# A kernel of ten transformer stages on one core: side steps ahead of the splits, one wait fewer at the eights' turns, and the first stage turning all of x before its tiles

## The chip, the cores and the metric

One core of a Trainium2 chip runs the whole program in one launch. The metric is the device time of an execution in microseconds (us). Three executions of the kernel before took 2540.09, 2541.14 and 2547.57 us; the median is 2541.14.

## The reference

x is 256 rows of 1024 float32 numbers. Two blocks work on it, of two layers each.

```python
def first_block(x, ...):          # DEPTH = 2
    for i in range(DEPTH):
        h = swiglu(rms_norm(x, g[0]), ffn_w_gate[i, 0], ffn_w_up[i, 0], ffn_w_down[i, 0])
        x = x + 0.5 * rms_norm(h, g[1])
        hm = rms_norm(x, g[2])
        m = dilated_attention(hm, ...) if i == 0 else retention(hm, ...)
        x = x + rms_norm(m, g[3])
        h = swiglu(rms_norm(x, g[4]), ffn_w_gate[i, 1], ffn_w_up[i, 1], ffn_w_down[i, 1])
        x = x + 0.5 * rms_norm(h, g[5])

def second_block(x, mem, ...):    # two layers
    for l in range(DEPTH):
        dq, dk, dv, c_q, c_kv_kr, xq, gate_logits = jnp.split(rmsnorm(x, g_mix[l]) @ w_in[l], ...)
        y_diff = diff_attention(dq, dk, dv, ..., diff_lambda[l], ...) @ w_diff_o[l]
        y_mla = latent_attention(c_q, c_kv_kr, ...) @ w_mla_o[l]
        y_mem = memory_cross_attention(xq, rmsnorm(mem, mem_gain[l]) @ w_mem_kv[l], ...) @ w_cross_o[l]
        merged = gates[:, :, 0] * y_diff + gates[:, :, 1] * y_mla + gates[:, :, 2] * y_mem
        x = x + merged @ w_out[l]
        x = x + jnp.square(jax.nn.relu(rmsnorm(x, g_mlp[l]) @ w_mlp1[l])) @ w_mlp2[l]
```

The dilated attention has 16 heads of 64 in three groups: the first is dense over a band, the second and third attend within classes of equal position modulo the dilation. The differential attention subtracts `lam` times its second map, and `lam` is computed from the small vector `diff_lambda`. The retention has 4 heads, each normed over its 512 values. All products are of float32 quality.

## The kernel before

**Tiles.** The weights are read in 744 tiles of 128 x 1024 float32 (512 KB). SyncE (SP) loads a tile into one of four raw buffers (L1504, L1511). ScalarE (ACT) rounds it to w_hi (L1780). VectorE (DVE, L2060), and in the mix stages every second time GpSimd (POOL, L2724), makes the rest, w_lo. TensorE (PE) then runs 12 matmuls of 512 columns for the tile: w_hi by x_hi, w_lo by x_hi, w_hi by x_lo, each four times (L1555 to L1557; L1579 to L1581 for blocks that go chunk by chunk). x itself is turned by PE in pieces of 128 (L1599) and divided into hi (ACT, L1806, L1808) and lo (DVE, L2086, L2088) in the same way.

**The plan.** The order of all work is written out once, as a list of steps, by Python generators. Every engine's program walks this one list and takes its part of each step, in order; an engine never passes a waiting instruction. The steps that matter here:

- `("mm", i)` and `("mm_chunk", i)`: PE's matmuls of tile i.
- `("split", i)`: ACT's w_hi and then w_lo of tile i, with SP's load of tile i+4. w_hi of tile i waits for the end of tile i-4 on PE, whose buffer it takes; the load of tile i+4 waits for w_lo of tile i.
- side steps: turning x or the heads, norms, rotations, scores, softmax, values. `drive(main, side)` runs one tile of `main` and then one group of side steps, in turn; `main` is a stage's projections. A tile's generator (`block()`, L552, and `block_by_chunk()`, L567) yields once a tile, and at that yield the side group is written into the list.
- `evac`: the result of a block is taken out of PSUM once its last tile is done.

`tile_used(i)` (L531) writes `("split", i + 4)`, or keeps it back while a stage ends. `second_part` is a function that the feed of a stage leaves behind: `block()` calls it after the stage's second tile.

**Stages.** ffn, dilated attention, ffn, ffn, retention, ffn, then mix, mlp, mix, mlp. `feed()` (L645) opens each: gains times x into `tok` (L2068), turned by PE, then rows' squares for the norm (ACT L1832). In its first half (`first`) it turns columns 0 to 511 of both halves of the rows, in the second (`second`) the others.

**The eights.** In the dilated stage the groups with classes go by eight heads (`by_classes()`, L915): scores on PE, softmax on DVE (L2260 to L2268) and ACT (exponential, L1905), den, the sum of the exponentials, on DVE (L2286), turns of the probabilities on PE (L1691), values on PE (L1711), weights and weighing, then `combine` and turns into `da_out_hi` (ACT L1806) and `da_out_lo` (DVE L2086). Two eights are interleaved. In the list den stands behind the softmax of the next half of the eight.

**Retention.** While the gates' and the output's tiles run, each head's values are normed with a chain DVE (L2430 to L2436), POOL (L2705), ACT, DVE (L2444).

**The prelude** (L1194) of a mix stage runs beside the last tiles of the stage ahead of it: the memory block and the small vectors are read by POOL's queue (L2819, L2825), then `lambda` computes lam on DVE and ACT (L2598 to L2604, L2019), and so on.

Of the kernel before, what the change touches and what calls it, by code (L numbers as in the profile page):

```python
# [49 lines left out]
RAW, SPLIT = 4, 4  # L50
# [339 lines left out]
class Kernel:  # L390
# [161 lines left out]
    def block(self, xt, w, rows, c0, n, first=0):  # L552
        view = w.rearrange("(k p) n -> p k n", p=P)
        chunks, per = rows // P, TILE // n
        b = self.new_block(xt, first, chunks, n)
        for k0 in range(0, chunks, per):
            nk = min(per, chunks - k0)
            self.tiles.append(Tile(view[:, k0:k0 + nk, c0:c0 + n], nk, n, b, k0))
            self.step("mm", len(self.tiles) - 1)
            self.tile_used(len(self.tiles) - 1)  # L560
            if self.second_part and len(self.tiles) == self.second_part[0]:
                self.second_part[1]()
                self.second_part = None
            yield
        return b

    def block_by_chunk(self, xt, w, rows, turned):  # L567
        view = w.rearrange("(k p) n -> p k n", p=P)
        b = self.new_block(xt, 0, rows // P, D)
        for k in range(rows // P):  # L570
            while not turned(k):
                yield
            self.tiles.append(Tile(view[:, k:k + 1, :], 1, D, b, k))
            self.step("mm_chunk", len(self.tiles) - 1)
            self.tile_used(len(self.tiles) - 1)
            yield
        return b

    def by_turns(self):
# [65 lines left out]
    def feed(self, between=None, order=""):  # L645
        st, g = self.st, self.next_gain()
        self.xt = Transposed(f"x{st}", *self.xt_parts)
        self.xt_scaled = True
        gained = {}

        def part(half, c):
            if self.pending:
                self.pending(half, c)
            by = "pool" if c and between else "dve"
            self.step("gain", st, half, c, by, g, [self.x_event[half][c]] + self.tok_after[half])
            gained[half, c] = "gain", st, half, c

        def turned(half, c):
            self.feed_turned = self.turn(lambda h, s: self.tok[:, h, s * P:(s + 1) * P], self.xt, half, [(4 * c + j, 4 * c + j) for j in range(4)],
                                         [gained[half, c]], self.xt_after, order=order)  # L660

        def first():
            turned(0, 0)
            turned(1, 0)

        def second():
            part(0, 1)
            part(1, 1)
            self.release(1)
            if between:  # L670
                between()
                first()
            turned(0, 1)
            turned(1, 1)
            self.release()
            self.pending = None
            self.step("next_gain", g + 2, list(gained.values()))
            self.tok_after = [[self.feed_turned]] * HALVES
            for half in range(HALVES):
                self.step("rows", st, half, list(self.x_event[half]), self.stat(2), self.stat(1), self.stat(1), "row_natural" if order else "row_scale")  # L680

        part(0, 0)
        part(1, 0)
        if between:
            second()
        else:
            first()
            if not self.tiles:
                for i in range(SPLIT):
                    self.split(i)  # L690
            self.second_part = len(self.tiles) + 2, second

    def last_tile(self):
# [828 lines left out]
def pe_program(k):  # L1522
    pe, q, ev = k.nc.tensor, Queue(k.nc.tensor), k.ev
# [8 lines left out]
    for what, *of in k.plan:  # L1532
# [6 lines left out]
        if what == "mm":  # L1539
            i, = of  # L1540
            t = k.tiles[i]
            b, hi, lo = t.block, k.w_hi[i % SPLIT], k.w_lo[i % SPLIT]
# [5 lines left out]
            for half in range(HALVES):  # L1548
                bank = banks.held["blk", b.uid, half][:, 0:t.n]
                for j in range(t.nk):  # L1550
# [6 lines left out]
                    mm = pe.matmul(bank, xl, wh, start=False, stop=(c == b.chunks - 1))  # L1557
# [6 lines left out]
        if what == "mm_chunk":  # L1564
            i, = of
            t = k.tiles[i]
            b, hi, lo = t.block, k.w_hi[i % SPLIT], k.w_lo[i % SPLIT]
# [5 lines left out]
            for c in range(2):  # L1573
                cols = slice(c * BLOCK, (c + 1) * BLOCK)
                for half in range(HALVES):
# [5 lines left out]
                    mm = pe.matmul(bank, xl, hi[:, cols], start=False, stop=(t.k0 == b.chunks - 1))  # L1581
# [6 lines left out]
        if what == "turn":  # L1588
# [9 lines left out]
            for j, (c, s) in enumerate(t.chunks):  # L1598
                mm = pe.transpose(bank[:, j * P:(j + 1) * P], src(t.half, s), order)  # L1599
# [4 lines left out]
        if what == "turn_heads":  # L1604
# [5 lines left out]
            for h in range(t.n):  # L1610
                for half in range(HALVES):
                    z = t.src(half, t.h0 + h)
                    at = h * SEQ + half * P
                    mm = pe.transpose(bank[0:z.shape[-1], at:at + P], z, order)  # L1614
# [51 lines left out]
        if what == "oct_scores":  # L1666
            o, = of
# [16 lines left out]
        if what == "oct_turn":  # L1684
            o, b = of
            bank = yield from bank_for("oct_turn", o.uid, b)
            q.wait_ge(*(yield from ev.of("oct_exp", o.uid, b)))
            q.wait_ge(*(yield from ev.of("oct_den", o.uid, b)))
            p = k.probs.held["oct", o.uid, b]
            for m in range(OCT // 2):  # L1690
                mm = pe.transpose(bank[:, m * P:(m + 1) * P], p[:, m * P:(m + 1) * P], k.ident[:, :])  # L1691
            mm.then_inc(*ev.mark(k.pe_done, ("oct_read", o.uid, b)))
            k.probs.give(ev.at["oct_read", o.uid, b], "oct", o.uid, b)
# [1186 lines left out]
```

## Time and profile before

| what | value |
|---|---|
| executions, median | 2540.09, 2541.14, 2547.57; 2541.14 us |
| the profiled execution | 2539.82 us, span 2538.5 us |
| mean granted TensorE clock | 0.982 |
| PE busy | 2421.2 us, 95% of the span, 11746 instructions |
| PE weight loads | 1957.6 us, 77% |
| DVE busy | 1480.2 us, 58% |
| ACT busy | 1194.4 us, 47% |
| POOL busy | 281.5 us, 11% |
| DMA | 411.36 MB, mean 162 GB/s |
| w_lo on DVE (L2060) | x688, 837.9 us, mean 1222 ns |
| w_lo on POOL (L2724) | x56, 134.3 us, mean 2399 ns |
| w_hi on ACT (L1780) | x744, 781.0 us, mean 1053 ns |

PE's matmuls overlap by their durations, so the distance of their starts, not the duration, is what one costs. The granted clock is a share of the full 2.4 GHz. An idle time in brackets is how long the engine had done nothing, with the instruction that ended it.

### The profile page before, as it was taken

How to read it: one execution, taken by the hardware profiler on the slowest of the kernel's cores; microseconds unless marked ns; L12 is line 12 of the kernel's file. 1: busy time of each engine (PE TensorE's matmuls, PEld its weight loads, DVE VectorE, ACT ScalarE, POOL GpSimd, SP SyncE). 2: the span in 40 equal slices, each digit the busy share in tenths (PEclk: the TensorE clock that was granted, in tenths of full speed). 3: DMA queues.
4: the chain of work that ended last, by engine and by line, in shares of the span. 5: the costliest groups of instructions: out<-in, count | busy, mean ns of one | idle time of the engine just before them, and what ended most of it. 6: DMA issues, size and time to landing. Idle time of an engine off the chain costs nothing.

```text
span 2538.5 us, 29689 instructions
## 1 busy us (share of the span) xinstructions
PE 2421.2 (95%) x11746; PEld 1957.6 (77%) x11746; DVE 1480.2 (58%) x2158; ACT 1194.4 (47%) x1754; POOL 281.5 (11%) x248
## 2 busy tenths in 40 slices
PE   7998999989999999999999999999999999999999
PEld 5786777768877877777787787777787877887787
DVE  4555556675555547766554577655565576645653
ACT  4443454344434445444444465554554455554543
POOL 1100010000000000000001112333101122333000
PEclk9998999989999999999999999999999999999999
DMA  6765544446556666544566554344556554445554
GB/s 206 204 182 151 175 119 117 144 122 190 175 173 184 181 182 181 160 141 144 176 184 182 181 170 143 108 125 158 179 175 209 179 160 123 117 131 159 169 174 146
DMA packets 211339, 411.36 MB, mean 162 GB/s; under 512 B 13690, under 2 KB 26890, under 8 KB 211200
## 3 DMA queue, kind: packets, MB, share of 16 engines
q1 hardware_dynamic: 204192, 388.55, 51.1%
q0 software_dynamic: 6576, 19.80, 2.9%
q8 instruction: 93, 1.52, 0.2%
q10 hardware_dynamic: 432, 1.11, 0.1%
q14 instruction: 46, 0.38, 0.1%
HBM read 408.31 MB, written 1.10 MB: 161 GB/s over the span
## 4 chain that ended last, share of the span: by engine, by line
PE 81%; DVE 11%; ACT 4%; DMA 2%; issue 2%; POOL 1%; ACTq 0%; DVEq 0%
PE banks L1555 24%; PE banks L1557 23%; PE banks L1556 23%; DVE w_lo L2060 3%; PE banks L1599 2%; ACT w_hi L1780 2%; PE banks L1649 2%; PE banks L1623 1%; PE banks L1634 1%; PE banks L1614 1%; DMA small<-in_diff_lambda 1%; POOL stat L2705 1%; DVE mx_merged L2693 1%; PE banks L1579 1%; PE banks L1580 1%
## 5 line engine op out<-in xcount | busy, mean ns | idle before, releaser
L2060 DVE TENSOR_TENSOR w_lo<-w_raw,w_hi 128x1024 fp32r<-128x1024 f32 x688 | 837.9, 1222 | 862.0 <-ACT w_hi L1780 859.2
L1780 ACT ACTIVATE w_hi<-w_raw 128x1024 fp32r<-128x1024 f32 (+2 forms) x744 | 781.0, 1053 | 974.6 <-PE banks L1557 922.5
L1555 PE MATMUL banks<-w_hi,xt_hi 128*128 128x512 f32 (+3 forms) x2112 | 848.2, 402 | 20.7 <-DVE xt_lo L2088 10.3
L1556 PE MATMUL banks<-w_lo,xt_hi 128*128 128x512 f32 (+3 forms) x2112 | 823.3, 390 | 0.0
L1557 PE MATMUL banks<-w_hi,xt_lo 128*128 128x512 f32 (+3 forms) x2112 | 822.5, 389 | 0.0
L1555 PEld LDWEIGHTS banks<-w_hi,xt_hi 128*128 128x128 f32 x2112 | 403.6, 191 | 111.3 <-issue 18.3
L1557 PEld LDWEIGHTS banks<-w_hi,xt_lo 128*128 128x128 f32 x2112 | 402.3, 190 | 89.1
L1556 PEld LDWEIGHTS banks<-w_lo,xt_hi 128*128 128x128 f32 x2112 | 403.6, 191 | 83.1 <-issue 3.1
L2705 POOL TENSOR_TENSOR stat<-stat,minus_half 128x1 f32<-128x1 f32 (+2 forms) x60 | 54.6, 916 | 1052.4 <-DVE stat L2147 731.3
L2724 POOL TENSOR_TENSOR w_lo<-w_raw,w_hi 128x1024 fp32r<-128x1024 f32 x56 | 134.3, 2399 | 304.4 <-ACT w_hi L1780 304.3
L1555 PE MATMUL banks<-w_hi,ffn_ht_hi 128*128 128x512 f32 x352 | 141.9, 403 | 3.3 <-DVE w_lo L2060 3.3
L1557 PE MATMUL banks<-w_hi,ffn_ht_lo 128*128 128x512 f32 x352 | 140.5, 399 | 0.0
L1556 PE MATMUL banks<-w_lo,ffn_ht_hi 128*128 128x512 f32 x352 | 140.5, 399 | 0.0
L1555 PE MATMUL banks<-w_hi,mlp_ht_hi 128*128 128x512 f32 x256 | 102.2, 399 | 1.2 <-DVE w_lo L2060 1.2
L1557 PE MATMUL banks<-w_hi,mlp_ht_lo 128*128 128x512 f32 x256 | 101.5, 396 | 0.0
L1556 PE MATMUL banks<-w_lo,mlp_ht_hi 128*128 128x512 f32 x256 | 101.4, 396 | 0.0
L1555 PEld LDWEIGHTS banks<-w_hi,ffn_ht_hi 128*128 128x128 f32 x352 | 67.0, 190 | 19.5 <-DVE w_lo L2060 3.7
L1557 PEld LDWEIGHTS banks<-w_hi,ffn_ht_lo 128*128 128x128 f32 x352 | 67.0, 190 | 16.4
L1556 PEld LDWEIGHTS banks<-w_lo,ffn_ht_hi 128*128 128x128 f32 x352 | 67.1, 191 | 15.8
L1599 PE MATMUL banks<-ident,tok 128*128 128x128 f32 x212 | 35.2, 312 | 39.4 <-DVE tok L2068 39.4
L1867 ACT ACTIVATE probs<-probs,mx_nmax 128x256 f32<-128x256 f32 x96 | 42.9, 448 | 63.0 <-DVE mx_nmax L2205 62.8
L1599 PEld LDWEIGHTS banks<-ident,tok 128*128 128x128 f32 x212 | 28.0, 159 | 47.1 <-issue 30.0
(382 smaller groups left out, 2550.0 us busy)
## 6 DMA issues: line engine op xcount, KB each, us to landing
w_raw<-in_w_mlp SPq DMA_DIRECT2D x128, 512.0 KB, 3.8
w_raw<-in_w_in SPq DMA_DIRECT2D x104, 512.0 KB, 3.7
w_raw<-in_ffn_w_gate SPq DMA_DIRECT2D x88, 512.0 KB, 3.7
w_raw<-in_ffn_w_up SPq DMA_DIRECT2D x88, 512.0 KB, 3.8
w_raw<-in_ffn_w_down SPq DMA_DIRECT2D x88, 512.0 KB, 3.7
w_raw<-in_attn_w_in SPq DMA_DIRECT2D x72, 512.0 KB, 3.8
w_raw<-in_ret_w_in SPq DMA_DIRECT2D x64, 512.0 KB, 3.9
w_raw<-in_ret_w_out SPq DMA_DIRECT2D x16, 512.0 KB, 3.9
```

Source lines behind the costliest of these rows:

```text
L1555: pe.matmul(bank, xh, wh, start=(c == 0), stop=False)
L1556: pe.matmul(bank, xh, wl, start=False, stop=False)
L1557: mm = pe.matmul(bank, xl, wh, start=False, stop=(c == b.chunks - 1))
L1579: pe.matmul(bank, xh, hi[:, cols], start=(t.k0 == 0), stop=False)
L1580: pe.matmul(bank, xh, lo[:, cols], start=False, stop=False)
L1599: mm = pe.transpose(bank[:, j * P:(j + 1) * P], src(t.half, s), order)
L1649: mm = pe.matmul(out[:, at:at + h.dv], pt[:, kh, s, :], h.v(kh), start=(kh == 0), stop=(kh == n_keys - 1))
L1780: act.activation(k.w_hi[i % SPLIT][:, 0:m], k.raw[i % RAW][:, 0:m], ACT.Copy).then_inc(*ev.mark(k.w_hi_made, ("w_hi", i)))
L1867: act.activation(row, row, ACT.Exp, bias=h.nmax[:, s:s + 1], scale=-1.0, accum_out=h.den[:, s:s + 1]).then_inc(*done)
L2060: dve.tensor_tensor(lo, raw, hi.bitcast(F32), ALU.subtract).then_inc(*ev.mark(k.w_lo_made, ("w_lo", i)))
L2705: pool.tensor_tensor(out, mean, k.minus_half[:, 0:n], ALU.pow).then_inc(*ev.mark(k.pool_done, name))
L2724: pool.tensor_tensor(lo, raw, hi.bitcast(F32), ALU.subtract).then_inc(*ev.mark(k.w_lo_pool, ("w_lo", i)))
```

## The change

In the blocks, the split of a tile is no longer written right behind its matmuls, but after the yield, so behind the side steps of that tile. Where `second_part` is called it stays where it was. In `feed()` of the first stage both parts of x are handled, and the rows' squares, ahead of splits 0 to 3 and of tile 0; before, the second part came after the second tile. PE's turn of an eight waits for the exponential alone; before, it waited for den as well.

```diff
--- before.py
+++ after.py
@@ -556,12 +556,16 @@
         for k0 in range(0, chunks, per):
             nk = min(per, chunks - k0)
             self.tiles.append(Tile(view[:, k0:k0 + nk, c0:c0 + n], nk, n, b, k0))
-            self.step("mm", len(self.tiles) - 1)
-            self.tile_used(len(self.tiles) - 1)
+            used = len(self.tiles) - 1
+            self.step("mm", used)
             if self.second_part and len(self.tiles) == self.second_part[0]:
+                self.tile_used(used)
                 self.second_part[1]()
                 self.second_part = None
-            yield
+                yield
+            else:
+                yield
+                self.tile_used(used)
         return b
 
     def block_by_chunk(self, xt, w, rows, turned):
@@ -571,9 +575,10 @@
             while not turned(k):
                 yield
             self.tiles.append(Tile(view[:, k:k + 1, :], 1, D, b, k))
-            self.step("mm_chunk", len(self.tiles) - 1)
-            self.tile_used(len(self.tiles) - 1)
+            used = len(self.tiles) - 1
+            self.step("mm_chunk", used)
             yield
+            self.tile_used(used)
         return b
 
     def by_turns(self):
@@ -683,11 +688,13 @@
         part(1, 0)
         if between:
             second()
+        elif not self.tiles:
+            first()
+            second()
+            for i in range(SPLIT):
+                self.split(i)
         else:
             first()
-            if not self.tiles:
-                for i in range(SPLIT):
-                    self.split(i)
             self.second_part = len(self.tiles) + 2, second
 
     def last_tile(self):
@@ -1685,7 +1692,6 @@
             o, b = of
             bank = yield from bank_for("oct_turn", o.uid, b)
             q.wait_ge(*(yield from ev.of("oct_exp", o.uid, b)))
-            q.wait_ge(*(yield from ev.of("oct_den", o.uid, b)))
             p = k.probs.held["oct", o.uid, b]
             for m in range(OCT // 2):
                 mm = pe.transpose(bank[:, m * P:(m + 1) * P], p[:, m * P:(m + 1) * P], k.ident[:, :])
```

## Rows read from the trace of the kernel before

**Rows 1.** Part 4 of the page, the chain that ended last: its shares by engine.

```profile
PE 81%; DVE 11%; ACT 4%; DMA 2%; issue 2%; POOL 1%; ACTq 0%; DVEq 0%
```

**Rows 2.** The list of waits, all engines: total us, times, longest us.

```profile
ACT w_hi L1780 <- PE banks L1557: 922.5, 582, 7.3
PE banks L1691 <- DVE da_den L2286: 12.5, 4, 4.9
```

**Rows 3.** Timeline at the start: start us, duration us, instruction, [idle before <- releaser].

```profile
16.76 0.80 PE L1555 MATMUL banks<-w_hi,xt_hi 128*128 128x512 f32 x1 [2.89 <-DVE w_lo L2060]
...
27.25 1.97 PE L1599 MATMUL banks<-ident,tok 128*128 128x128 f32 x8 [3.07 <-DVE tok L2068]
29.75 0.62 ACT L1832 ACTIVATE junk<-x 128x512 bf16<-128x512 f32 x1
29.87 0.76 PE L1555 MATMUL banks<-w_hi,xt_hi 128*128 128x512 f32 x1 [0.65 <-DVE xt_lo L2088]
```

**Rows 4.** Timeline of PE, the eights in the dilated stage.

```profile
414.16 0.63 PE L1691 MATMUL banks<-ident,probs 128*128 128x128 f32 x4 [2.88 <-DVE da_den L2286]
...
427.77 0.63 PE L1691 MATMUL banks<-ident,probs 128*128 128x128 f32 x4 [1.44 <-DVE da_den L2286]
...
509.89 1.12 PE L1691 MATMUL banks<-ident,probs 128*128 128x128 f32 x4 [4.87 <-DVE da_den L2286]
...
523.71 0.76 PE L1579 MATMUL banks<-w_hi,da_out_hi 128*128 128x512 f32 x1 [3.87 <-DVE da_out_lo L2086]
```

**Rows 5.** Timeline of DVE, between the last two of these.

```profile
504.69 1.23 DVE L2060 TENSOR_TENSOR w_lo<-w_raw,w_hi 128x1024 fp32r<-128x1024 f32 x1 [1.49 <-ACT w_hi L1780]
...
510.81 1.23 DVE L2060 TENSOR_TENSOR w_lo<-w_raw,w_hi 128x1024 fp32r<-128x1024 f32 x1 [0.98 <-ACT w_hi L1780]
```

**Rows 6.** Timeline of PE, end of the retention stage.

```profile
1188.51 0.39 PE L1579 MATMUL banks<-w_hi,re_yt_hi 128*128 128x512 f32 x1
1188.74 0.39 PE L1580 MATMUL banks<-w_lo,re_yt_hi 128*128 128x512 f32 x1
...
1196.14 0.50 PE L1579 MATMUL banks<-w_hi,re_yt_hi 128*128 128x512 f32 x1 [1.41 <-DVE w_lo L2060]
```

**Rows 7.** Timeline of DVE, end of the retention stage.

```profile
1189.40 1.23 DVE L2060 TENSOR_TENSOR w_lo<-w_raw,w_hi 128x1024 fp32r<-128x1024 f32 x1 [1.79 <-ACT w_hi L1780]
...
1194.86 1.22 DVE L2060 TENSOR_TENSOR w_lo<-w_raw,w_hi 128x1024 fp32r<-128x1024 f32 x1 [1.79 <-ACT w_hi L1780]
```

**Rows 8.** Timeline of PE, end of the last ffn stage, with the first prelude.

```profile
1389.88 0.80 PE L1555 MATMUL banks<-w_hi,ffn_ht_hi 128*128 128x512 f32 x1 [3.29 <-DVE w_lo L2060]
```

**Rows 9.** Timeline of DVE, the same stretch.

```profile
1376.53 1.23 DVE L2060 TENSOR_TENSOR w_lo<-w_raw,w_hi 128x1024 fp32r<-128x1024 f32 x1 [1.59 <-ACT w_hi L1780]
1386.77 0.29 DVE L2598 TENSOR_TENSOR lam_products<-small 128x128 f32<-128x128 f32 x1 [9.01 <-DMA small<-in_diff_lambda]
```

**Rows 10.** Windows of 4 us: busy us (x instructions) by engine, PEclk, DMA share, GB/s.

```profile
1376.00:1380.00 4.00, 4.00 (x19) 3.22 (x18) 1.23 (x1) 1.78 (x2) 2.91 (x6) 1.00 0.96 254
1390.00:1394.00 4.00, 4.00 (x10) 3.14 (x11) 4.00 (x11) 2.74 (x6) 0.00 (x0) 0.50 0.66 203
```

**Rows 11.** Timeline of PE, end of the first mlp stage, with the second prelude.

```profile
1917.97 0.50 PE L1555 MATMUL banks<-w_hi,mlp_ht_hi 128*128 128x512 f32 x1 [1.21 <-DVE w_lo L2060]
```

**Rows 12.** Timeline of DVE, first mix stage, rotation of q.

```profile
1515.23 0.68 DVE L2572 TENSOR_TENSOR tmp<-mx_q,rope_q 128x512 f32<-128x512 f32 x1
...
1522.10 0.68 DVE L2580 TENSOR_TENSOR mx_q<-mx_q,tmp 128x512 f32<-128x512 f32 x1
```

**Rows 13.** Timeline of PE, first mix stage.

```profile
1521.14 0.40 PE L1555 MATMUL banks<-w_hi,xt_hi 128*128 128x512 f32 x1
...
1530.23 0.47 PE L1555 MATMUL banks<-w_hi,xt_hi 128*128 128x512 f32 x1 [1.57 <-DVE mx_k L2531]
...
1581.97 0.52 PE L1634 MATMUL banks<-ident,probs 128*128 128x128 f32 x3 [2.17 <-DVE mx_kcat L2625]
...
1659.53 0.63 PE L1634 MATMUL banks<-ident,probs 128*128 128x128 f32 x4 [1.26 <-ACT probs L1876]
```

## Prediction

> **What bounds the kernel now.** I read the page first, then the waits, then the timelines of each place where TensorE stands still. In the chain of waits [rows 1] the reader is to see that PE carries 81% and that VectorE (DVE) comes next with 11%: nearly all of the span is matmul columns that the change leaves alone, and only places where another engine hands over late can move. In the list of waits [rows 2] two lines matter. ScalarE (ACT) stood 922.5 us before its w_hi, each time for a tile to end on PE. That is no loss by itself, since a split that waits for tile i makes tile i+4, more than 8 us ahead of use. But whatever stands behind such a split on ACT and DVE is held for up to a tile (2.8 us: 12 matmuls, 0.23 us apart [rows 6]), then for ACT's 1.05 us and DVE's 1.22 us. The other line is PE's 12.5 us in four waits for da_den at the eights' turns. All gaps of PE of 0.25 us or more that I found in its timeline add up to about 108 us. Some 41 of these are at the ends of stages, where no side step stands, and 11 at the start before x is there. So what is to be had is some 55 us at most, and I go through these gaps.
>
> **The rule of the change.** The old order is tile i, split i+4, side steps, tile i+1, split i+5. The new one is tile i, side steps, split i+4. Two things follow. A side step is no longer behind split i+4, but it is now followed by split i+4, whose wait (end of tile i) is met earlier than that of split i+5: side chains gain up to 1.05 + 1.22 = 2.3 us of latency, plus what their engine idled for PE. And each w_lo moves behind one more group of side steps: where DVE and ACT are full of side work, w_lo of tile n comes about when w_lo of n+1 came before. In the long ffn and mlp bodies DVE waits for ACT, w_lo has more than 5 us to spare, and I cost the edit at nothing; without that cover each late w_lo would cost its own delay.
>
> **Start** (old: tile 0 at 16.76, a wait of 3.07 for the second half's turns, those 1.97, another 0.65, tile 2 at 29.87 [rows 3]). New: the second half's gains on DVE right after the first half's xt_lo (15.25 to 16.6), turns until 18, their hi and lo until 19.3, ACT's four squares (the first is in [rows 3]; each 0.62 and then 0.19 for its sum, a little overlapped, 3.0 us for four), then w_hi 0 at about 22 to 22.8 and w_lo 0 at 24.1. Tile 0 at 24.1 instead of 16.76; tiles 0 and 1 plus the mended gaps fill that, and tile 3 comes at 34.4 instead of 34.6. **-0.2**, bounds -0.7 (squares ahead of the turns' hi) and +1 (half clock twice).
>
> **Eights in the dilated stage.** All four den waits vanish as named. What is late next? First pair (2.88 and 1.44 [rows 4]): the values of the first eight wait for da_v, which DVE and ACT evacuate at about 433.0, against 434.5 where PE stood: **-1.4** (bounds -4.3, all of it, and +0.5). Second pair: PE is 3.4 us ahead at 488, loses 2.4 of it again at the next scores, which need da_kt (about 495.7 against 496.7), and then goes through the turn at 509.89 [rows 4] without its 4.87. It gains nothing by that, since at 523.71 it waits for da_out_lo anyway, by the same DVE chain: softmax, combine, weights, turns' lo. In that chain DVE idles only 1.49 at 504.69 and 0.98 at 510.81 [rows 5]; no DVE instruction goes away. At best the chain ends 1.0 (earlier scores) + 2.5 (those idles) = 3.5 us earlier. But between these steps now stand w_lo's whose w_hi ACT makes behind an exponential (0.63 + 1.05), which is the same sum as before: **+0.2** (bounds -3.5 and +1.5). The half clock behind 509.89 may go or stay; PE's wait at 523.71 absorbs it. Together -1.2. If DVE's order did not bind, the 12.5 would all come back with about 3.5 of half clock.
>
> **End of retention.** DVE's chain of a head's norm lasts 5.46 us (w_lo 1189.40 to w_lo 1194.86 [rows 7]) and has one w_lo in it. Now tile 346 (PE 1188.51 [rows 6]) gets the place of 1189.40 and is ready at 1190.6; tile 347 (1191.3, twelve matmuls on) that of 1194.86, ready 1196.1; tile 348, which waited 1.41 until 1196.14 [rows 6], is ready at about 1198.5. Less 1.2 that the chain gains at its start, less what is absorbed: **+2.2**, bounds 0 (chain ahead by a whole split) and +3.5 (with the half clock after a longer wait).
>
> **Lambda in the prelude, twice.** DVE's lam_products waits 9.01 us for its DMA until 1386.77 [rows 9]. Ahead of it stood w_lo 1376.53, for tile 409, which PE ran until 1386.6; behind it w_lo of tile 410, for which PE waited 3.29 us, until 1389.88 [rows 8]. Now lambda is ahead of split 409. Queued behind the waiting instruction are then w_lo 409 and, by ACT's lam, w_hi 409, and PE waits for them: tile 409 starts at about 1389.9 and tile 410 a tile later. One tile of 2.8 us more is lost; the half clock is paid in both. Second layer: the wait of 1.21 [rows 11] becomes 4.0, again +2.8, and now it is long enough for what happened after 3.29: granted clock 0.50, which is the level of 1.2 GHz, and 10 matmuls in 4 us instead of 19 [rows 10], at most 2.5 us for a tile, of which I take 2.0. **+7.6**; bounds +3 and +9. The lower one: the load that follows w_lo 409 is held back too, so the DMA may land up to 2.1 us sooner (a tile of 524 KB at 254 GB/s [rows 10]) in each layer. I take none of it: the reading of the memory block (1 MB, issued just before) is in flight beside it in any case.
>
> The DMA share was 0.96 in 1376 to 1380 while lambda was on its way [rows 10]. The Trainium skill, DMA: Bandwidth & Descriptors, section "Issuing engines are not separate DMA queues", says that transfers of all issuing engines end up on the same 16 DMA engines and interleave. By that rule, which the share of 0.96 fits, the withheld load makes lambda earlier by the full 2.1 us in each layer, the second layer's half clock goes as well, and my sum would be about -5 instead of +1.2; by the row alone it stays at +1.2. It would not leave "no change".
>
> **Mix: q and k turning.** Six rotation instructions for each half, two halves from 1515.23 to 1522.10 + 0.68 [rows 12], stand now ahead of a w_lo instead of behind it. Tile 453, at 1521.14 [rows 13], gets its w_lo at about 1522.3: +1.2. Tile 461 in the same manner for k: +1.6. PE waits at 1530.23 (1.57 [rows 13]) and 1558.52 for DVE's mx_k and mx_v, which the same chain brings no later, so most is given back: **+0.6 a layer, +1.2** (bounds -1 and +5).
>
> **Mix attention.** Early gaps (2.17 at 1581.97 [rows 13], 0.52, 1.70) hang on a chain of norms through DVE, POOL and ACT, and lose about one split's latency between them: -1.0 a layer, **-2.0** (bounds -8.8 and +1). Late gaps (five a layer, first 1.26 at 1659.53 [rows 13], sum 3.5) wait for an exponential whose maximum stood behind a w_lo that DVE idled for; a 2.3 us shorter way covers each: -3.2 a layer, **-6.4** (bounds -7 and 0).
>
> **Sum.** -0.2 - 1.2 + 2.2 + 7.6 + 1.2 - 2.0 - 6.4 = **+1.2 us** on the profiled execution (2539.82, span 2538.5), which is 1.3 below the median 2541.14: I add to the median, **2542.3**. Within 0.3% (7.6 us) is about what a measurement of this kernel can't tell from no change.
>
> **Rivals.**
> Gains hold: side work really was held by splits, so the den waits (12.5 + 3.5 half clock), early gaps (8.8) and late gaps (6.4) all go, and lambda costs 3: 3 - 31.2 = -28, some 2513; half of it gives 2527. For: DVE is busy only 58%. Against: DVE is nearly continuous there [rows 5], and da_out_lo, not da_den, is the last wait there. It decides if the wait at 523.71 shrinks below 3.
>
> Late w_lo (the other sign): w_lo behind DMA and DVE chains, lambda 9, retention 3.5, rotations 5, and of the late gaps only half comes back (-3.2), the eights nothing: +14, 2555. For: w_lo's slack [rows 6, 8] is zero already. Against: such places are few. It decides from about 8 us of new PE<-w_lo waits that no gap gives back.
>
> Nothing moves: every freed wait turns into the next one and the lambda DMA lands earlier: 2541, within 1.
>
> **Chances.** Forecast 0.42, nothing 0.13 (together the same: 0.55); gains 0.25; late w_lo 0.20. Range: 2527 to 2552, one in ten beyond each end; the forecast's own is 2535 to 2548.
>
> **What would show it.** After: no waits PE<-da_den, but a wait of PE for da_out_lo of about 8 us near 523, and one for da_v or values near 433; PE waiting for w_lo about 6 us near 1387 and 4 near 1915, with half clock after both; two or three short waits near 1190 to 1198; the five late gaps of each mix layer gone; tile 0 at 24.1. Wrong would be: the wait for da_out_lo not longer than 4 (gains hold), lambda's wait ahead of no tile, or new w_lo waits in the bodies.

## The result, and the profile after

The changed kernel takes 2530.03 us (median of 4 executions, 2527.24 to 2531.84) against 2542.35 for the kernel before: ratio 0.995, 95% interval [0.9935, 0.9966], so 12 us or 0.5% faster. Run again later as an experiment of its own it gave 2531.00 us and 0.9953 [0.9939, 0.9967]. The forecast was no change (2542.3, with 0.25 for faster). The time is inside the range of 2527 to 2552, but it moved 12 us down where 1.2 us up was forecast.

The profiled execution after took 2531.84 us (span 2530.5), 8.0 less than the profiled one of before. It is the slowest of its kernel's four, and that of before (2539.82) lies 2 us below the medians of that kernel (2541.49 to 2542.35 in all comparisons): this is where the other 4 us are. So the two traces can account for 8 us of the 12. The chain of waits has moved a little from PE [rows 1] to the other engines:

```profile
PE 2417.6 (96%) x11746; PEld 1958.9 (77%) x11746; DVE 1484.7 (59%) x2158; ACT 1189.6 (47%) x1754; POOL 285.0 (11%) x248
...
PE 79%; DVE 12%; ACT 5%; issue 1%; DMA 1%; POOL 1%; ACTq 0%; DVEq 0%; POOLq 0%
```

The list of waits of the changed kernel, in the columns of [rows 2]. ACT stands 176 us less for a tile's end, no wait for den is left, and PE's waits for w_lo have grown from 11.2 us in four (first line, of the kernel before) to 20.2 in eight, the 5.8 at the start among them:

```profile
PE banks L1555 <- DVE w_lo L2060: 11.2, 4, 3.8
...
ACT w_hi L1786 <- PE banks L1564: 746.9, 472, 7.0
PE banks L1562 <- DVE w_lo L2066: 20.2, 8, 5.8
PE banks L1586 <- DVE da_out_lo L2092: 4.5, 1, 4.5
PE banks L1688 <- DVE da_kt L2124: 3.0, 1, 3.0
PE banks L1717 <- DVE da_v L2108: 2.4, 1, 2.4
```

The timeline of PE where the prediction had its terms: start and eights (to set beside [rows 3, 4]), end of retention [rows 6], the two preludes [rows 8, 11], the first mix stage [rows 13].

```profile
23.31 0.80 PE L1562 MATMUL banks<-w_hi,xt_hi 128*128 128x512 f32 x1 [5.83 <-DVE w_lo L2066]
...
429.76 1.16 PE L1717 MATMUL banks<-da_v,probs_t 64*64 64x64 f32 x64 [2.37 <-DVE da_v L2108]
...
490.46 1.99 PE L1688 MATMUL banks<-da_kt,da_qt 64*64 64x64 f32 x64 [3.02 <-DVE da_kt L2124]
...
506.94 1.11 PE L1606 MATMUL banks<-flip,tok 128*128 128x128 f32 x4 [2.44 <-DVE tok L2363]
...
517.21 0.76 PE L1586 MATMUL banks<-w_hi,da_out_hi 128*128 128x512 f32 x1 [4.52 <-DVE da_out_lo L2092]
...
1184.48 0.51 PE L1586 MATMUL banks<-w_hi,re_yt_hi 128*128 128x512 f32 x1 [1.43 <-DVE w_lo L2066]
...
1379.12 0.50 PE L1562 MATMUL banks<-w_hi,ffn_ht_hi 128*128 128x512 f32 x1 [3.80 <-DVE w_lo L2066]
...
1513.07 0.51 PE L1562 MATMUL banks<-w_hi,xt_hi 128*128 128x512 f32 x1 [0.90 <-DVE w_lo L2066]
...
1538.60 0.50 PE L1562 MATMUL banks<-w_hi,xt_hi 128*128 128x512 f32 x1 [1.11 <-DVE w_lo L2066]
...
1574.30 0.52 PE L1641 MATMUL banks<-ident,probs 128*128 128x128 f32 x3 [2.34 <-ACT probs L1873]
...
1906.81 0.79 PE L1562 MATMUL banks<-w_hi,mlp_ht_hi 128*128 128x512 f32 x1 [2.78 <-DVE w_lo L2066]
```

Set against the prediction's signs: the four den waits are gone, but da_out_lo waits 4.52 and not about 8; the w_lo waits at lambda are 3.80 and 2.78, not 6 and 4; at the end of retention there is one short wait, not two or three; tile 0 is at 23.31 (24.1).

Both kernels run the same 744 tiles in the same order, so the start of each tile can be compared. I did that for all traces, and took out what the half clock costs (matmuls of 512 columns 0.427 us apart instead of 0.233: their number times 0.194), since the stretches at a granted clock of 0.50 differ from one execution to the next: the same kernel traced twice has 23.9 and 21.0 us of it. Differences to before in us; "half" is the half clock of the whole trace counted in this way, 25.0 before. The predicted +4.8 has 2.0 of half clock in it.

| stretch, tiles | predicted | den alone | first stage alone | order alone | whole change | again |
|---|---|---|---|---|---|---|
| start, 0 to 3 | -0.2 | -0.5 | +0.4 | -0.5 | +0.3 | +0.2 |
| eights, 100 to 139 | -1.2 | -2.7 | +1.9 | -2.4 | -3.8 | -3.7 |
| end of retention, 311 to 349 | +2.2 | +0.1 | +0.1 | -1.6 | -1.6 | -1.7 |
| lambda, first, 405 to 429 | +2.8 | -1.1 | -1.4 | +0.2 | +0.1 | +0.6 |
| lambda, second, 550 to 589 | +4.8 | -0.1 | +0.4 | +1.6 | +1.9 | +1.4 |
| q and k, 430 to 467 and 590 to 627 | +1.2 | +2.1 | -0.4 | +2.1 | +2.1 | +2.1 |
| early attention, 467 to 482 and 627 to 642 | -2.0 | +0.3 | +1.5 | -0.2 | +0.5 | -0.3 |
| late attention, 482 to 493 and 642 to 653 | -6.4 | 0.0 | 0.0 | -6.7 | -6.7 | -6.7 |
| whole trace (sum, where predicted) | +1.2 | -1.8 | +2.4 | -7.5 | -6.8 | -8.3 |
| half | | 24.6 | 25.6 | 27.7 | 23.9 | 21.0 |

The columns of the two small edits show how far this can be trusted, since most rows hold places that they don't touch. Retention and late attention are steady to 0.1. The other rows are not. The count leaves out narrower matmuls: the +2.1 of den alone at q and k is the granted clock of 0.50 from 1556 to 1562 in that trace, where before and after have 1.00, and not the late w_lo that the order brings there. The eights of first stage alone (+1.9) have a stretch at 0.50 from 412 to 416, where before has 1.00, which makes a part of it. The first lambda moves with the landing of its DMA, as shown below; what moves early attention by 1 to 2 us is not shown.

### The profile page after: what moved, and what is told of

Read it like the earlier page. It is cut to its first block, busy times and chain, and to the rows that moved or that the text cites. A ratio compares the mean times of both kernels' runs of the same rounds, so it can differ in the third digit from the quotient of the medians.

```text
span 2530.5 us, 29568 instructions
## 1 busy us (share of the span) xinstructions
PE 2417.6 (96%) x11746; PEld 1958.9 (77%) x11746; DVE 1484.7 (59%) x2158; ACT 1189.6 (47%) x1754; POOL 285.0 (11%) x248
## 4 chain that ended last, share of the span: by engine, by line
PE 79%; DVE 12%; ACT 5%; issue 1%; DMA 1%; POOL 1%; ACTq 0%; DVEq 0%; POOLq 0%
PE banks L1562 23%; PE banks L1564 23%; PE banks L1563 23%; DVE w_lo L2066 3%; PE banks L1606 3%; ACT w_hi L1786 2%; PE banks L1656 1%; PE banks L1630 1%; PE banks L1621 1%; PE banks L1641 1%; DVE mx_merged L2699 1%; PE banks L1586 1%; DVE norm_sums L2499 1%; DMA small<-in_diff_lambda 1%; PE banks L1588 1%
```

## The experiments

All times are medians; the ratio is to the kernel before, which ran beside each.

| kernel | us | ratio, 95% interval |
|---|---|---|
| den wait removed alone | 2535.49 | 0.9976 [0.9967, 0.9986] |
| first stage alone | 2539.14 | 0.9987 [0.9978, 0.9996] |
| order alone | 2534.90 | 0.9979 [0.9969, 0.9989] |
| order and den | 2530.20 | 0.9965 [0.9953, 0.9978] |
| whole, small vectors first | 2529.42 | 0.9950 [0.9937, 0.9962] |
| whole, lambda after the split | 2525.30 | 0.9931 [0.9918, 0.9943] |
| whole, rotations after the split | 2526.02 | 0.9937 [0.9925, 0.9949] |
| whole, short den | 2529.28 | 0.9944 [0.9931, 0.9958] |
| whole, retention in the old order | 2530.54 | 0.9959 [0.9945, 0.9972] |
| whole, dilated stage in the old order | 2531.21 | 0.9960 [0.9946, 0.9973] |
| whole, again | 2531.00 | 0.9953 [0.9939, 0.9967] |
| whole, lambda and rotations after the split | 2521.48 | 0.9920 [0.9905, 0.9935] |

### The three parts of the change

> The kernel before with one edit: PE's turn of an eight doesn't wait for den. Theory A (the order of side steps ahead of splits brings nearly all of the gain; the eights are bound by DVE's chain, and PE gives back most of what the four den waits of 12.5 us take): 1 to 3 us faster than before, the waits moving to da_v, da_kt and da_out_lo. Theory B (the 5.2 us that the trace of the changed kernel gains between tiles 111 and 139 come from the den waits): 5 us faster, whatever the order.

```diff
-            q.wait_ge(*(yield from ev.of("oct_den", o.uid, b)))
```

Measured: 6.0 us faster, [-8.4, -3.6], of which 2.7 stand at the eights in its trace: 3.0 less at the first pair (tiles 100 to 131) and 0.2 more at the second. The timeline of PE there:

```profile
432.12 1.16 PE L1710 MATMUL banks<-da_v,probs_t 64*64 64x64 f32 x64 [1.23 <-DVE da_v L2101]
...
493.90 1.98 PE L1681 MATMUL banks<-da_kt,da_qt 64*64 64x64 f32 x64 [4.38 <-DVE da_kt L2117]
...
510.30 0.69 PE L1599 MATMUL banks<-flip,tok 128*128 128x128 f32 x4 [3.57 <-DVE tok L2356]
...
520.59 0.47 PE L1579 MATMUL banks<-w_hi,da_out_hi 128*128 128x512 f32 x1 [4.39 <-DVE da_out_lo L2085]
```

The waits move to da_v, da_kt, tok and da_out_lo as theory A has it, 13.6 us here against 16.4 of before (12.5 for den and 3.87). But it keeps more than A allowed, and its median is nearer to B. The trace shows less than the median: its execution is 2.1 us above it, and that of before 1.7 below its own. So 3.8 of the 6.0 us are in neither trace and can't be placed.

> The kernel before with one edit: side steps stand ahead of the split of their tile, in all stages; den wait and first stage as before. Theory A: 6 to 10 us faster than before; within 3 us of the whole change. In the trace, the waits for w_lo at the end of the retention stage and at lambda look as in the whole change, and the five late gaps of each mix stage are gone. Theory B: at most 5 us faster, and the eights as slow as before.

```diff
             self.step("mm", used)
...
-            self.tile_used(used)
             yield
+            self.tile_used(used)
```

Measured: 6.6 us by the medians, 5.3 by the ratio, -7.5 us in the trace without half clock. As theory A has it, the late gaps of each mix stage are all but gone (those left are of 0.3 us or less): -3.36 in each layer. Against A, it is 5 us from the whole change and not within 3. Against both theories, the eights gained 2.4 too, though the den wait was still there: 1.2 at each pair. So den and order each give about 2.5 of the same 4.

> The whole change without its edit of the first stage. Theory A and B: as the whole change, some 8 to 12 us faster than before. Rival C: 2 us or more off that.

Measured: 2530.20, as the whole change by the median, yet with a ratio that is 0.0015 higher; the two intervals overlap. Together with

> The kernel before with one edit: the first stage turns all of x, and computes the rows' squares, ahead of splits 0 to 3 and tile 0. Both theories: no difference that can be measured, tile 3 within 0.5 us of before (34.56) although tile 0 starts 6.5 us later. Rival C (the first stage carries a part of the gain, by a longer or shorter half clock): 2 us or more either way.

```diff
+        elif not self.tiles:
+            first()
+            second()
+            for i in range(SPLIT):
+                self.split(i)
```

which is 0.9987 [0.9978, 0.9996], the first stage likely carries some 2 to 3 us, as rival C has it, though of these two only the run with the first stage alone is clear of no difference. Tile 3 is no earlier for it (34.58 in this trace, 34.56 before). What differs is the half clock in the first 71 tiles: 6.0, 7.0, 6.4 and 6.2 us in the four traces with the old first stage, 2.9 to 4.1 in the ten with the new one. PE's long waits stand all ahead of tile 0 now (the last is the 5.83 us at 23.31) instead of on both sides of it, and the second stretch of half clock, at 27 to 34 us before, is not there. Why the opening of the second stage, at 226 and 243, also has less of it (3.3, 4.7, 2.3, 3.3 against 1.4 to 2.5) is not settled by these runs.

### Lambda

> The whole change, but at the step lambda alone the split of its tile stands ahead, as in the kernel before. Theory A (with lambda ahead of split 409 the load of tile 413 is held back, and lambda lands 2.3 us sooner for that: 8.8 us after its issue against 11.1): here the landing takes 11 us again in the first layer; PE waits for the tile after, not for this one, in layer 0 as long as before (about 3.3 us), in layer 1 about 1.2 instead of 2.78 and without half clock, so 2 to 4 us faster than the changed kernel. Theory B (the landing's length is chance, or the extra tile of stall doesn't exist): landing 8 to 9 us, and the time within 1 us of the changed kernel's.

```diff
+        self.flush()          # writes the split of the tile that has just been used
         self.step("lambda", layer, lam, 0.8 - 0.6 * math.exp(-0.3 * layer))
```

Measured: 4.7 us faster than the changed kernel (5.7 than its second measurement). PE's waits for w_lo at the two preludes, with DVE's lam_products ahead of the first:

```profile
1376.32 0.29 DVE L2614 TENSOR_TENSOR lam_products<-small 128x128 f32<-128x128 f32 x1 [6.89 <-DMA small<-in_diff_lambda]
1379.43 0.51 PE L1572 MATMUL banks<-w_hi,ffn_ht_hi 128*128 128x512 f32 x1 [1.17 <-DVE w_lo L2076]
...
1904.17 0.50 PE L1572 MATMUL banks<-w_hi,mlp_ht_hi 128*128 128x512 f32 x1 [0.59 <-DVE w_lo L2076]
```

The tile of stall that the prediction charged is real: 3.80 and 2.78 become 1.17 and 0.59, and the half clock behind both goes (7 and 12 matmuls after, none here). But theory A's landing was wrong: 8.94 us in the first layer, not 11. All 14 traces together say what the landing (from issue to DVE's first use) depends on. With the load of the next tile let through, in five traces, it is 8.9 to 11.1 us in the first prelude (median 9.7) and 8.4 to 9.4 in the second (8.9); with the load held back and the order of issue as before, in eight, 8.2 to 9.3 (8.5) and 7.5 to 7.9 (7.8). So a load held back comes with about 1.1 us in each layer, about half of the 2.1 that its bytes would be, and the first layer's 11.06 of before was the longest of all, on which I had put a whole term.

> The whole change, and POOL issues the five small vectors (lambda's among them) ahead of the memory block of 1 MB, not behind it. Theory A (the price of the change at lambda is DVE's wait for its DMA, which is long because the memory block's packets are ahead of it): lambda lands within 5 us of its issue instead of 8.8 and 7.7, PE's waits for w_lo of 3.80 us and 2.78 us and the half clock behind the second go away, and the kernel is 6 to 9 us faster than the changed one, about 2522. Theory B (all transfers share 16 engines, so that the order of issue hardly matters): lambda lands within 1.5 us of where it did, and the time within 2 us of the changed kernel's.

```diff
-            pool.dma_start(mem[:, :, :], a["mem_2"][0]...)
             for n, (name, size) in enumerate(SMALL.items()):
...
+            pool.dma_start(mem[:, :, :], a["mem_2"][0]...)
```

Measured: 2529.42, the changed kernel's time. POOL's issue and DVE's first use, for the first layer:

```profile
1367.69 0.54 POOL L2830 DMA_DIRECT2D small<-in_diff_lambda  x1
1376.41 0.29 DVE L2604 TENSOR_TENSOR lam_products<-small 128x128 f32<-128x128 f32 x1 [8.78 <-DMA small<-in_diff_lambda]
```

8.72 us, and 9.22 in the second layer, against 8.76 and 7.73: theory B. Being issued behind the memory block isn't what makes these vectors slow. Whether the block slows them at all is not shown: issued half a microsecond later it is still in flight beside them, and now takes 10.8 and 11.2 us itself instead of 8.7 and 6.7. No run leaves it out.

### Rotations

> The whole change, but the rotations of q and k of the differential attention stand behind the split of their tile, as before. Theory A: PE's waits for w_lo at tiles 453 and 461 (0.90 and 1.11, and the same in the second mix layer) go, and what they cost comes back: 2 to 3 us in all by the trace. Theory B: they take the place of waits for mx_k and mx_v, which come back as they go (1.57 and 1.10 before): within 1 us of the changed kernel's.

```diff
+            self.flush()
             return self.turning(heads[:, :, 0:n], heads[:, :, n:], four, ...)
```

Measured: 4.0 us faster than the changed kernel by the medians, and in the trace 1.9 us less in each of the two stretches (q and k: -0.6 and -1.0 to before, instead of +1.3 and +0.8). Theory A. Behind a rotation group of twelve instructions on DVE (7.5 us [rows 12]) a w_lo is late. For q the delay is given back, as predicted: mx_k's wait of 1.57 is gone in the changed kernel. For k it isn't: mx_v's wait of 1.10 shrank to 0.95 only. And here mx_k's wait is 0.44 without any late w_lo: the new order elsewhere is worth 1.14 us a layer between tiles 451 and 463, and the late w_lo turns that into a loss of 0.72.

### Retention and eights, undone

> The whole change, but the retention stage keeps the old order (split ahead of side steps). Theory A (the new order shortens the norm chain more than it delays w_lo, 1.6 us in the trace between tiles 311 and 348): 1.6 us slower than the changed kernel by the trace, with DVE's waits of 2.95 us for w_hi back in the chain of each head. Theory B (what my prediction held: w_lo one chain step later costs 2.2 us here): 2 us faster than the changed kernel.

```diff
+            if self.stages[self.st][0] == "retention":
+                self.tile_used(used)
+                yield
...
```

Measured: 2530.54, too close to tell by the time; in the trace tiles 311 to 349 take exactly what they took before, 1.64 more than in the changed kernel. Theory A. DVE's timeline, first of the changed kernel, then of this one:

```profile
1171.56 1.22 DVE L2066 TENSOR_TENSOR w_lo<-w_raw,w_hi 128x1024 fp32r<-128x1024 f32 x1 [1.79 <-ACT w_hi L1786]
...
1177.74 1.23 DVE L2066 TENSOR_TENSOR w_lo<-w_raw,w_hi 128x1024 fp32r<-128x1024 f32 x1 [1.79 <-ACT w_hi L1786]
...
1183.20 1.23 DVE L2066 TENSOR_TENSOR w_lo<-w_raw,w_hi 128x1024 fp32r<-128x1024 f32 x1 [1.79 <-ACT w_hi L1786]
```

```profile
1177.05 1.23 DVE L2073 TENSOR_TENSOR w_lo<-w_raw,w_hi 128x1024 fp32r<-128x1024 f32 x1 [2.95 <-ACT w_hi L1793]
...
1183.23 1.23 DVE L2073 TENSOR_TENSOR w_lo<-w_raw,w_hi 128x1024 fp32r<-128x1024 f32 x1 [1.79 <-ACT w_hi L1793]
...
1188.68 1.23 DVE L2073 TENSOR_TENSOR w_lo<-w_raw,w_hi 128x1024 fp32r<-128x1024 f32 x1 [1.79 <-ACT w_hi L1793]
```

With the old order one w_lo in each head waits 2.95 for its w_hi, with the new one all wait 1.79. What ACT does ahead of that w_hi is in its timeline, first of this kernel (for the w_lo at 1177.05), then of the changed one (for the w_lo at 1171.56):

```profile
1174.82 1.26 ACT L1977 ACTIVATE re_g<-banks,row_scale 128x512 f32<-128x512 f32 x2
1175.95 1.06 ACT L1793 ACTIVATE w_hi<-w_raw 128x1024 fp32r<-128x1024 f32 x1
```

```profile
1170.48 1.05 ACT L1786 ACTIVATE w_hi<-w_raw 128x1024 fp32r<-128x1024 f32 x1
1171.43 1.26 ACT L1970 ACTIVATE re_g<-banks,row_scale 128x512 f32<-128x512 f32 x2
```

In the old order ACT takes the gates of a head (re_g) out of PSUM ahead of w_hi, since that `evac` stands between the side step and the next tile's split; in the new order w_hi comes first. The w_lo's of successive heads are 31.49 us apart before and 30.33 after.

> The whole change, but the dilated stage keeps the old order; the turns still don't wait for den. Theory A (at the eights the gain is the den wait's, about 4 us by the trace of it alone, and the order adds about 1): tile 139 at most 1.5 us later than in the changed kernel. Theory B (order and den wait gain only together): tile 139 is 3 us or more later.

The same edit with "dilated". Measured: 2531.21. The eights' stretch is -2.2 to before without half clock, 1.6 less gain than the whole change's -3.8; tile 139 is 1.24 later. Theory A, if barely, and its share for the order was too small. The loss is at the second pair alone (+0.8 instead of -1.3); the first is at -3.0 against -2.5.

> The whole change, but den sums only 8 of 64 exponentials for each row, so that DVE's reduce takes about 0.2 us instead of 0.68. Left out: the rest of each denominator. Theory A (DVE's chain in order bounds the eights since the den waits went): tile 139 is 2 to 3 us earlier than in the changed kernel, as the waits before da_kt, tok and da_out_lo shrink by 0.5 us for each den ahead of them. Theory B (the latency between engines bounds them, DVE has room): tile 139 within 0.7 us of the changed kernel.

```diff
-... .rearrange("p (m s j) -> p m s j", s=2, j=OF_CLASS), AX.X, ALU.add)
+... .rearrange("p (m s j) -> p m s j", s=2, j=OF_CLASS)[:, :, :, 0:8], AX.X, ALU.add)
```

The kernel leaves out 56 of the 64 exponentials of each sum; a den takes 0.21 us instead of 0.68. Measured: the stretch of the eights is 2.1 us shorter than in the changed kernel with half clock taken out (-5.9 against -3.8 to before), but in this execution 1.2 us more of half clock ate a part, so that tile 139 is 0.66 earlier. PE's rows there:

```profile
489.31 1.49 PE L1688 MATMUL banks<-da_kt,da_qt 64*64 64x64 f32 x64 [2.56 <-DVE da_kt L2124]
...
515.63 0.77 PE L1586 MATMUL banks<-w_hi,da_out_hi 128*128 128x512 f32 x1 [3.96 <-DVE da_out_lo L2092]
```

against 490.46 and 517.21. By the tile's time, the sign that was set down, this is theory B, just within its 0.7. The stretch without half clock speaks for A: eight other traces with the same order and no den wait have -3.7 to -4.1 there, this one -5.9. Two of the three waits named shrank by 0.5 (da_kt 3.02 to 2.56, da_out_lo 4.52 to 3.96), that for tok grew by 0.4. So DVE's chain bounds the eights at least in part.

### A version that beats both

> The whole change, with the old place of the split at two steps: behind tiles with lambda, and with the rotations of q and k of the differential attention. Theory A (w_lo late is paid only where DVE is held long ahead of it, and these are the places): the two gains add up, 7 to 9 us faster than the changed kernel, about 2522, some 20 us faster than before. Theory B (the second gain is given back as PE comes earlier to the next stage's waits): no better than either alone, about 2525.

Measured: 2521.48 (2519.32 to 2522.75), ratio 0.9920 [0.9905, 0.9935]: theory A. The two gains add up (4.7 and 4.0, together 8.5 to 9.5), 20 us or 0.8% off the kernel before. Its trace has a landing of 10.4 us at the first lambda and so shows little gain there; with a landing like the others' it would be about 2 us faster still, by my estimate from -0.3 in these tiles here and -2.3 with lambda alone behind the split.

> The changed kernel itself, to have it beside the others with as many runs, and a second trace of it. All theories: 2530 us, and a trace that differs from the first by the lengths of the stretches at half clock alone.

Measured: 2531.00, and traces that differ by 2.9 us in half clock and, against what was expected, by 1.5 us in the rest (early attention and lambda).

## Why the prediction was wrong, step by step

**The failed steps are three terms of the sum, all on one side: eights, end of retention, first lambda.** They were forecast at -1.2, +2.2 and +2.8 and measured at -3.8, -1.6 and +0.1: off by 2.6, 3.8 and 2.7 us, 9.1 together, where 8.0 us separate the sum (+1.2) from what is measured without half clock (-6.8) and 9.5 in the second trace; the other errors nearly cancel. The half clock, 1.1 and 4.0 us less than before, comes on top.

*Eights*. First pair ("**-1.4**"): the den waits gave more than that. Den alone has -3.0 there, since PE's values, which wait for da_v, came at 432.12 in that trace (431.6 in the time of before), not at 433.0; the new order takes 0.5 of it back (-2.5). Second pair ("+0.2"): for the den wait alone this was right (+0.2 in its trace), and that DVE's chain binds was right too. What failed is that the order would give the chain nothing. DVE's timeline of before and then of after, from a w_lo to the last da_out_lo of the first turn:

```profile
484.36 1.23 DVE L2060 TENSOR_TENSOR w_lo<-w_raw,w_hi 128x1024 fp32r<-128x1024 f32 x1 [1.49 <-ACT w_hi L1780]
...
522.95 1.12 DVE L2086 TENSOR_TENSOR da_out_lo<-banks,da_out_hi 128x256 fp32r<-128x256 f32 x2
```

```profile
477.88 1.23 DVE L2066 TENSOR_TENSOR w_lo<-w_raw,w_hi 128x1024 fp32r<-128x1024 f32 x1 [1.57 <-ACT w_hi L1786]
...
516.45 1.13 DVE L2092 TENSOR_TENSOR da_out_lo<-banks,da_out_hi 128x256 fp32r<-128x256 f32 x2
```

38.59 and 38.57 us: this piece of chain did not change at all. But its beginning is 6.48 earlier while PE's tiles around it are 4.75 earlier, a lead of 1.7 us. The same w_lo with the den wait removed alone, and with the order alone:

```profile
481.98 1.22 DVE L2059 TENSOR_TENSOR w_lo<-w_raw,w_hi 128x1024 fp32r<-128x1024 f32 x1 [1.49 <-ACT w_hi L1779]
```

```profile
482.56 1.22 DVE L2065 TENSOR_TENSOR w_lo<-w_raw,w_hi 128x1024 fp32r<-128x1024 f32 x1 [1.56 <-ACT w_hi L1785]
```

2.38 earlier where PE is 2.39 earlier, and 1.80 where PE is 0.06: the lead comes with the order and only with it. Before, the softmax that opens this chain (480.01) stands behind the w_lo at 478.87, which waits 2.00 for its w_hi; after, it (474.10) waits for its scores on PE alone. I took the start of the chain from one hand-over (da_kt, 1.0) and did not carry this forward. The sign of 8 us for da_out_lo failed for another reason: it is 4.39 with den alone too, since da_kt and tok hold PE up ahead of it (4.38 and 3.57).

*End of retention* ("+2.2"). I moved each w_lo one place down in the old timeline and let the chain start 1.2 earlier. The chain itself got faster, by the 2.95 that became 1.79, once in each head. The w_lo at 1183.20 has the place of the one at 1194.86 [rows 7], 11.66 earlier, where PE is 8.4 earlier: the chain has gained 3.2 on PE. So the late w_lo is there (PE waits 1.43 for tile 347, which is 1.6 late), but tile 346 isn't late at all, and tile 348, which waited 1.41 before, gives the 1.6 back. Ahead of it 0.3 and 1.4 are gained, the larger one where PE's wait of 1.16 for re_g at 1166.07 is gone. The step took the shape of the old timeline as fixed.

*First lambda* ("One tile of 2.8 us more is lost"). For an equal landing that is nearly right: the changed kernel and the one with lambda behind the split land at 8.76 and 8.94 and have +0.1 and -2.3 in the tiles 405 to 429, 2.4 apart. What failed is that I let both kernels land after 11.06 us, the longest landing of all traces. In the two that have lambda as before and landed after 9.67 (den alone, first stage alone) this stretch is 1.1 and 1.4 us shorter than in the trace of before. Of the 2.3 between 11.06 and 8.76 about 1.1 is what comes with the load held back, and the rest is the luck of one execution. The Trainium skill, DMA: Bandwidth & Descriptors, section "Issuing engines are not separate DMA queues", has the transfers of all issuing engines share the same 16 DMA engines. These runs agree in direction, with 1.1 us where my estimate from the rate was 2.1.

**What held.** Late attention: -3.2 a layer forecast, -3.36 measured. The second pair of eights without the order, +0.2. Second lambda: +4.8 forecast; +1.9 and 2.3 of half clock make 4.2 in the first trace (+1.4 and none in the second). Start: -0.2 against 0.3. Tile 453 was late by 1.07 (1.2 forecast) and 461 by 1.28 (1.6), and what is left of both is +0.7 a layer (+0.6). den's waits vanished and others took their place.

**What was off without deciding.** q and k +2.1 instead of +1.2, with 0.7 of it in the tiles behind the rotations. Early attention about 0 instead of -2.0; it isn't the late q and k, since it is -0.5 and +0.1 in the two kernels that have the rotations behind their split, so the cause stays open. The half clock I counted only where I saw a wait appear; the first stage changed it by 2 to 3 us. And I had argued the whole from one execution, though three times alone (2540.09 to 2547.57) told that an execution moves by several microseconds.

"Nothing moves" is refuted. "Late w_lo" named places that exist: putting two of them back gave 8.5 us. But they were paid for by the gains. "Gains hold" was nearest by the number (2527 at half), not by its mechanism: its own sign, the wait at 523.71 below 3, did not come (4.52), and early attention gave nothing. That the time fell inside the range is owed to this rival's half, not to the sum.

## What to carry to other kernels

In an in-order plan, put short side steps ahead of work that waits for the bottleneck engine, and long ones, or ones that wait for a DMA, behind it: that order was worth 5 to 7 us here, and putting two kinds of steps back behind their splits another 9. When a chain's wait is shortened, follow the chain from its first link and let its lead add up; moving instructions one place down in the old timeline counts the costs and misses the gains. Take a DMA's landing from several traces before a term rests on it.

## What was not expected of the hardware

Lambda's vector (128 KB as it is broadcast) takes 7.5 to 11.1 us from issue to first use in the two preludes of 14 traces, and no less (8.72, 9.22) when it is issued ahead of the block of 1 MB.

The clock behind a wait is not a fixed price: after waits of 3.80 and 3.44 us at the same tile (409) the first matmul is once at the full spacing and once at half, and the stretches at half clock cost 20 to 30 us over a whole execution, by the 512-column matmuls alone. Executions of one kernel are spread over 10 us (before: 2536.91 to 2547.57), with a mean granted clock of 0.982 to 0.985 in those under 2538 and 0.979 to 0.981 in those over 2546.
